# Hybrid attention layer on Trainium2: twelve gate projections move into the stick-breaking groups and pass through HBM, three into the last differential group

## The reference, cut to what matters

```python
proj = jnp.einsum('bsd,de->bse', x, w_in[l])          # 5120 columns = 40 tiles of 128
# columns: qa, ka, va (8 heads), qb, kb, vb (4 heads), gate a (1024), gate b (1024)
ya = _stick_breaking_attention(qa, ka, va)            # sigmoid scores, reversed running product, times v
q1, q2 = _rope(qb[:, :, 0], cos, sin), _rope(qb[:, :, 1], cos, sin)   # and k1, k2
yb = _differential_attention(q1, q2, k1, k2, vb, lam) # softmax(z1) - lam * softmax(z2), times v
yb = _rms_norm(yb, subln_gain[l]) * (1.0 - lam_init)
gate_a = jax.nn.sigmoid(proj[..., c_vb:c_ga])
gate_b = jax.nn.sigmoid(proj[..., c_ga:])
merged = (gate_a * jnp.einsum('bse,ed->bsd', ya, w_branch_a[l])
          + gate_b * jnp.einsum('bse,ed->bsd', yb, w_branch_b[l]))
mix_out = jnp.einsum('bsd,de->bse', merged, w_out[l])
x = _layer_norm(DEEPNORM_ALPHA * x + mix_out, ln1_gain[l], ln1_bias[l])
h = jnp.square(jax.nn.relu(jnp.einsum('bsd,df->bsf', x, w_ff1[l])))
x = _layer_norm(DEEPNORM_ALPHA * x + jnp.einsum('bsf,fd->bsd', h, w_ff2[l]), ln2_gain[l], ln2_bias[l])
```

## Time and profile before

| what | value |
|---|---|
| device time, median of 3 runs | 1707.2 us (1705.44 to 1707.46) |
| profiled execution, first to last instruction | 1700.1 us |
| PE busy in it | 1582.8 us, 93% |
| DVE, ACT, POOL busy | 956.7, 493.3, 458.0 us |
| granted TensorE clock, mean | 0.984 of full speed |

### The profile page before, as it was taken

One profiled execution on the slowest core, in us unless ns is written; L12 is line 12 of the kernel. 1 busy time (PEld: TensorE's weight loads), 2 busy tenths in 40 slices (PEclk: granted clock), 3 DMA queues, 4 the chain that ended last, 5 costly groups with the idle time before them and its releaser, 6 DMA issues.

```text
span 1700.1 us, 21123 instructions
## 1 busy us (share of the span) xinstructions
PE 1582.8 (93%) x7472; PEld 1293.1 (76%) x7472; DVE 956.7 (56%) x1536; ACT 493.3 (29%) x897; POOL 458.0 (27%) x264
## 2 busy tenths in 40 slices
PE   8888887788889889999999999999999999999996
PEld 6666666666777778888878888888888888888885
DVE  3898897988677673121135664444444444444548
ACT  3555565665555442000022221111111111111121
POOL 3544444433222210222230032222222222222313
PEclk9999999999999999999999999999999999999999
DMA  4100100001000000212133131111111111111102
GB/s 162 45 13 26 38 25 13 25 13 38 14 25 25 25 16 23 62 38 59 44 107 99 41 111 47 50 50 50 49 49 49 49 49 49 49 49 49 50 1 99
DMA packets 95209, 79.79 MB, mean 47 GB/s; under 512 B 3248, under 2 KB 85168, under 8 KB 95024
## 3 DMA queue, kind: packets, MB, share of 16 engines
q1 hardware_dynamic: 95152, 79.05, 14.9%
HBM read 74.84 MB, written 4.19 MB: 46 GB/s over the span
## 4 chain that ended last, share of the span: by engine, by line
PE 66%; DVE 16%; issue 12%; POOL 3%; ACT 1%; DMA 1%; DVEq 0%; SPq 0%; POOLq 0%; ACTq 0%
PE p_z L848 6%; PE p_z L850 6%; PE p_z L849 6%; PE p_proj L497 4%; PE p_proj L495 4%; PE p_proj L493 4%; PE p_proj L826 3%; PE p_proj L827 3%; PE p_proj L828 3%; DVE a_t L1205 3%; PE p_z L769 2%; PE p_z L770 2%; PE p_z L771 2%; PE p_z L698 2%; PE p_z L699 2%
## 5 line engine op out<-in xcount | busy, mean ns | idle before, releaser
L493 PE MATMUL p_proj<-xt_h,w_hi 128*128 128x512 f32 x640 | 256.3, 401 | 0.6 <-DVE xt_l L1205 0.6
L497 PE MATMUL p_proj<-xt_h,w_lo 128*128 128x512 f32 x640 | 255.0, 398 | 0.0
L495 PE MATMUL p_proj<-xt_l,w_hi 128*128 128x512 f32 x640 | 253.3, 396 | 0.0
L1594 DVE TENSOR_TENSOR res<-p_z,res 128x512 f32<-128x512 f32 x224 | 150.8, 688 | 109.9 <-PE p_z L850 109.9
L1665 POOL TENSOR_TENSOR w_lo<-w_raw,w_hi 128x1024 fp32r<-128x1024 f32 x48 | 116.6, 2430 | 322.0 <-DVE w_hi L1212 322.0
L1756 POOL TENSOR_TENSOR w_l<-w_raw,w_h 128x1024 fp32r<-128x1024 f32 x31 | 79.5, 2585 | 366.2 <-DVE w_h L1562 366.2
L849 PE MATMUL p_z<-w_l,h_h 128*128 128x512 f32 x448 | 174.3, 389 | 0.0
L850 PE MATMUL p_z<-w_h,h_l 128*128 128x512 f32 x448 | 174.3, 389 | 0.0
L848 PE MATMUL p_z<-w_h,h_h 128*128 128x512 f32 x448 | 174.3, 389 | 0.0
L497 PEld LDWEIGHTS p_proj<-xt_h,w_lo 128*128 128x128 f32 x640 | 122.2, 191 | 23.2
L493 PEld LDWEIGHTS p_proj<-xt_h,w_hi 128*128 128x128 f32 x640 | 122.2, 191 | 22.3 <-DVE xt_l L1205 0.6
(11 more groups left out here) (270 smaller groups left out, 3226.0 us busy)
## 6 DMA issues: line engine op xcount, KB each, us to landing
w_raw<-w_ff SPq DMA_DIRECT2D x64, 512.0 KB, 4.0
w_raw<-w_in SPq DMA_DIRECT2D x40, 512.0 KB, 3.8
y<-x SPq DMA_DIRECT2D x8, 512.0 KB, 8.5
wo_raw<-w_out SPq DMA_DIRECT2D x8, 512.0 KB, 8.0
rows<-x SPq DMA_DIRECT2D x8, 512.0 KB, 3.3
out<-rows_out SPq DMA_DIRECT2D x8, 512.0 KB, 2.6
w_raw<-w_branch_a SPq DMA_DIRECT2D x8, 256.0 KB, 2.8
w_raw<-w_branch_b SPq DMA_DIRECT2D x8, 256.0 KB, 3.2
```

What stands on the lines that cost most here:

```text
L493: pe.matmul(o, w_hi[n_slot][:, k, :], xt_h[:, k, cols], start=(k == 0), stop=False)
L495: pe.matmul(o, w_hi[n_slot][:, k, :], xt_l[:, k, cols], start=False, stop=False)
L497: mm = pe.matmul(o, w_lo[n_slot][:, k, :], xt_h[:, k, cols], start=False, stop=(k == KT - 1))
L1594: dve.tensor_tensor(o, by_block(dn_banks[n % 4]), o, ALU.add).then_inc(dn_added, 1)
```

## The change

A group now has six filler tiles if it is an SB group: the three that the next group needs and three gate tiles. The six halves of those gate tiles go through a sigmoid on ACT (`gate_half`) into three new buffers `gst`, and SP stores each finished gate, 512 KB, to an HBM scratch of twelve rows (`store_gate`). These are gates a and b of column tiles 2 to 7. The last DF group gets three filler tiles (gates a0, b0, a1), and one gate (b1) is left to cover the norm of yb (`last_gate`). In stage 3 the branches follow each other directly; SP brings the stored gates back (`load_gates`), DVE splits the branch weights three column tiles ahead (`split_branch`) over three slots. All counts that the semaphores wait for are rewritten.

```diff
     def tile(self, t):
-        return self.g * 3 + (3 + t)
+        return self.g * 6 + (3 + t) if self.sb else self.g * 3 + (15 + t)
...
+            def store_gate(g, j):
...
+                sp.dma_start(gate_rows[bass.ds(g * 3 + j, 1)].rearrange("a p c -> (a p) c"), gst[j][:, :])\
+                  .then_inc(s_gst, 16)
...
+            def load_group(g, gate_col, qkv_col, store=True):
+
+                for t in range(6):
+                    load_tile(g * 6 + (3 + t), qkv_col(t) if t < 3 else gate_col(t - 3))
+                    if store and 1 <= t < 4:
+                        store_gate(g - 1, t - 1)
...
+            def load_gates(i):
+
+                if i == 2:
+                    sp.wait_ge(s_gst, 12 * 16)
+                    sp.wait_ge(rp_done, 16)
+                else:
+                    sp.wait_ge(m_ready, i - 2)
+                for t in range(2):
+                    sp.dma_start(gate_pairs[i % 3][t][:, :], gate_rows[6 * t + i - 2]).then_inc(gate_in[i % 3], 16)
+
+            load_branch(0)
+            load_branch(1)
+            load_gates(2)
+            for i in range(2, KT):
                 load_branch(i)
-                load_tile(i * 3 + 27, i * P + (GATE_A + P))
-                load_tile(i * 3 + 28, i * P + (GATE_B + P))
-            load_branch(KT - 1)
+                if i + 1 < KT:
+                    load_gates(i + 1)
...
-            attention(Group(0, True, 3, False))
+            attention(Group(0, True, 6, False))
             with pe.Fori(1, SB_GROUPS - 1) as g:
-                attention(Group(g, True, 3, False))
-            attention(Group(SB_GROUPS - 1, True, 3, True))
+                attention(Group(g, True, 6, False))
+            attention(Group(SB_GROUPS - 1, True, 6, True))
...
-            attention(Group(GROUPS - 1, False, 2, False))
+            attention(Group(GROUPS - 1, False, 3, False))
...
-            with pe.Fori(1, KT - 2) as i:
-                branch(i, False, 0)
-                branch(i, False, 1)
-                gates(i)
-            gates(KT - 2)
-            for i in (KT - 2, KT - 1):
+            for i in range(1, KT):
                 branch(i, False, 0)
                 branch(i, False, 1)
...
+                def gate_half(t, h):
+
+                    act.wait_ge(pj_done, G.tile(t) * 2 + (h + 1))
+                    if h == 0 and not (isinstance(g, int) and g == 0):
+                        act.wait_ge(s_gst, g * 48 + 16 * (t - 5))
+                    act.activation(gst[t - 3][:, h * NH:(h + 1) * NH], p_proj[:, h, :], ACT.Sigmoid)\
+                       .then_inc(pj_plain, 1)
...
+            split_branch(2)
+            for i in range(KT - 1):
+                merge(i)
+                if i + 3 < KT:
+                    split_branch(i + 3)
```

More of the change, by code:

```diff
@@ L229, in layer_kernel @@
         x1t_l = at("x1t_l", 96, [P, KT, S], F32R)
-        gate_pairs = [stage[:2], [stage[2], at("gate_b1", 160, [P, S])]]
+        gst = [at(f"gst{j}", 207 + 4 * j, [P, S]) for j in range(3)]
+        gate_pairs = [stage[:2], gst[:2], [gst[2], at("gate_b1", 160, [P, S])]]
         m_h = [at(f"m_h{s}", 176 + 8 * s, [P, KT, P], F32R) for s in range(2)]
@@ L296, in layer_kernel @@
             sem("gate_ready"), sem("br_done"), sem("br_read"), sem("m_ready"))
+        s_gst = sem("s_gst")
+        gate_in = [sem(f"gate_in{j}") for j in range(3)]
         s_gain1, s_gain2 = sem("s_gain1"), sem("s_gain2")
@@ L357, in tile_after @@
         def tile_after(G, k):
-            done = [i // 2 for i in G.halves_at(k) if i in (1, 3)]
+            done = [i // 2 for i in G.halves_at(k) if i % 2 and i < 2 * G.tiles - 1]
+            assert len(done) < 2
             return done[0] if done else None
@@ new lines, in _ @@
+            load_group(0, lambda j: GATE_A + P * (2 + j), lambda t: P + SB_W * t, False)
+            with sp.Fori(1, SB_GROUPS - 1) as g:
+                load_group(g, lambda j: g * (5 * P) + (GATE_A + P * j), lambda t: g * P + (P + SB_W * t))
+            sp.dma_start(cs[:, :, :], rope).then_inc(s_rope, 16)
+            load_group(SB_GROUPS - 1, lambda j: GATE_A + P * (13 + j), lambda t: SB_W * (3 + t))
+            for t in range(3):
+                load_tile(27 + t, P + SB_W * (3 + t))
+                if t:
+                    store_gate(SB_GROUPS - 1, t - 1)
@@ L701, in branch, with last_gate @@
                 mm.then_inc(br_done, 1)
-            def gate(i, t):
+            def last_gate():
+                pe.wait_ge(wt_lo, 40)
                 for h in range(2):
[L706 to L714, removed]
+                    pe.wait_ge(pj_plain, 61 + h)
+                    yield from half_matmuls(0, h, lambda mm: mm.then_inc(pj_done, 1))
             pe.wait_ge(ya_split, 4)
             branch(0, True, 0, lambda: square_sums([3]))
-            next_gate = gate(0, 0)
+            next_gate = last_gate()
             for h in range(4):
@@ L957, in free @@
                                     act.wait_ge(st_pool, g * 2 + 2)
-                            plain(G.tile(t), h, stage[t], free)
+                            if t >= 3:
+                                gate_half(t, h)
+                            else:
+                                plain(G.tile(t), h, gst[0] if G.last and t == 2 else stage[t], free)
+                def gate_half(t, h):
[4 more added lines that the diff above has]
+                       .then_inc(pj_plain, 1)
                 def weights_om(u):
@@ L1083, in _ @@
                 act.activation(y_h[:, 4 + h, :], y[:, 4 + h, :], ACT.Copy).then_inc(yb_hi, 1)
[L1085 to L1095, removed]
-                        act.activation(gate_pairs[par][t][:, h * NH:(h + 1) * NH], p_proj[:, h, :], ACT.Sigmoid)\
-                           .then_inc(pj_plain, 1)
-            gates(0, 1)
-            with act.Fori(1, KT // 2 - 1) as j:
-                gates(j * 2 - 1, 0)
-                gates(j * 2, 1)
-            gates(KT - 3, 0)
-            gates(KT - 2, 1)
+            for h in range(2):
+                act.wait_ge(pj_done, 79 + h)
+                if h == 0:
+                    act.wait_ge(s_gst, 16 * 11)
+                act.activation(gst[1][:, h * NH:(h + 1) * NH], p_proj[:, h, :], ACT.Sigmoid).then_inc(gate_ready, 1)
+            for t, tile in enumerate((stage[0], stage[1], gst[0])):
+                act.wait_ge(pj_plain, 58 + 2 * t)
+                act.activation(tile[:, :], tile[:, :], ACT.Sigmoid).then_inc(gate_ready, 1)
             def wo_high(k):
@@ L1492, in _ @@
             wo_low(6)
-            merge(KT - 1, 1, 0, False)
+            merge(KT - 1)
             dve.wait_ge(mt_hi, 1)
```

151 lines of the change are left out of this document (80 added, 71 removed).

## The result

The changed kernel takes 1627.9 us (median of 4 runs, 1624.28 to 1630.42), the kernel before 1706.3 us (4 runs, 1702.29 to 1707.46): a ratio of 0.955, 95% interval 0.9528 to 0.9571. In a later round, with 5 runs of the changed kernel and 9 of the kernel before, the ratio was 0.9537 (0.9520 to 0.9554). The direction was as forecast, the size was not: 57 us were forecast, 78 came, and 1627.9 lies under the range of 1635 to 1673. The profiled execution has a span of 1623.9 us, 76.2 less than before and 19 under the 1643 that were forecast. The other 3 us of the 22 by which 1627.9 misses 1650 come from the step from span to median: 7.1 us were added, and here it is 4.0.

The account below looks back on a forecast made before the run. PE bounds the kernel, with waits on DVE's `a_t` in SB groups to fill. 54 (SB waits) + 5 (last DF group) - 4 (stage 3) + 2 (clock) = 57 us off 1700.1, span 1643, median 1650; range 1635 to 1673 us.

Parts of the forecast that it names:

- What leaves stage 3: Stage 3: 13 gate tiles of 10.88 us leave, 141.4 us off the path, 130.6 of them to SB groups.
- What comes into the SB groups: SB groups: three gate tiles each, 32.6 us of PE work, soak up waits; 54 us gained net of moved work.
- The worth of a wait: SB groups: 55 listed waits on `a_t`, 53.6 us, plus 0.16 us hidden under each, are worth 62.4 us.
- The waits left over: SB groups: 2 us of waits stay per group, 8 in all, where POOL subtractions and long scans meet.
- The clock: Third and fourth SB groups: part of PE's reduced clock returns with fewer waits, 2 us gained, bounds 0 and 5.
- The side work: SB groups: casts and POOL subtractions raise DVE's load from 69.5 to at most 78.7 us, counted on DVE, not PE.
- The last DF group: Last DF group: one more tile of 10.9 us, with 5 of 7 us of PE waits gone.
- Stage 3 as it is now: Stage 3: load and merge rounds take 10.8 to 12.8 us against PE's 10.88; five rounds cost 4 us.
- A: SB groups: a chain inside each batch keeps half the waits, 31 us gained instead of 54, 1673 us; chance 0.15.
- B: Stage 3: bound by its loads, 13 us lost instead of 4, 1659 us, or 1664 at slower loads; chance 0.10.
- D: SB groups and stage 3: DVE's casts stand waiting for weights, slower kernel, 1764 us at 6.7 us each; chance 0.05.
- C: SB and last DF groups: waits go entirely and the clock comes back, 74 us gained, 1633 us; chance 0.10.

Follow-up runs that it names:

- The doses: Kernel before plus 35, 70, 95 or 145 matmuls by a zero weight tile in each SB group's filler: 1707.8, 1706.2, 1722.0, 1757.5 us.
- zero dose of 145: Kernel before plus 145 matmuls by a zero weight tile in each SB group's filler, without casts, subtractions, sigmoids or stores: 1757.5 us.
- At five: Changed kernel with branch weights first, last merge moved up, and five filler tiles in SB groups 1 to 3, four in DF groups 1 to 3: 1621.2 us.

## Why the prediction was wrong

**What bounds the kernel**: right in kind. The waits on `a_t` were what the filler could take, and they went. They were not all of it.

**What leaves stage 3**: right, 141.4 - 4 forecast, 137.7 measured between the first and last branch matmul.

**What comes into the SB groups**: this is the step that failed. It took what filler can soak up as the listed waits on `a_t` with 0.16 us each, 62.4 us, and put at nothing what PE loses without a row for it. Forecast was that 54 of the 62.4 us of waits are saved, and 2 of clock. Measured, by lengths: 3 x (77.6 + 32.7 - 93.6) + (86.7 + 32.7 - 98.3) = 71.2 us, 15.2 more.

- *The worth of a wait*, the main term: PE lost 77 us at the turns and not 62.4. The 0.16 us were right for the first wait of a turn. Left out were the second one, of the values on `y_sum`, and waits of the transposes too short to be listed. With them 10.2 us more went than the listed waits say, 8.1 and 2.1. The doses show it without any of the change's other parts: it goes with PE work alone.
- *The waits left over*, taken at 2 us per group, 8 in all: 3.7 us listed in 7 places, with the hidden part 4.8, and nearly all in the fourth group. 3.2 us of the miss.
- *The clock*, taken at 2 us: 0.98 and 0.96 in the third and fourth group became 1.00 and 1.00, and the groups without their turns took 3.3 us less in all, 1.3 of the miss. Whether the clock alone would have won even that is not shown. The third group before was no longer than the first two (77.6 us each) though its matmuls took 1.6 us more, since it waited less, 16.6 us at its turns against 18.0 and 18.1. The prediction's bound of 5.0 us counts its 1.5 in full.

Together 14.7 of the 15 us. My bound of 62.4 for "nothing left" was no bound, since it stood on the listed time; that is why the range ended at 1635. PE's own side of a group, put at 96.2 us, fell with it: the first three groups are 93.6 and not 96 to 100. The fourth, 98.3, is in its range.

**The side work**: DVE's load in a group was forecast at up to 78.7 us and is 76 to 78. The sum came out, but its parts are not the forecast ones. The zero dose of 145 has 67.5 to 68 there, so three tiles add some 9.3 us. The six casts take 6.4 us instead of 2.1 for three, 4.3 more and not 2.1, since one of them in each group now stands beside a subtraction of POOL (`k_lo`) and takes four times as long:

```profile
226.12 2.77 DVE L1252 CAST w_hi<-w_raw 128x1024 fp32r<-128x1024 f32 x1
```

```profile
225.45 2.89 POOL L1730 TENSOR_TENSOR k_lo<-stage,k_hi 64x1024 fp32r<-64x1024 f32 x1 [1.80 <-DVE k_hi L1260]
```

The other 5.0 us are DVE's remaining operations, less than the 3 x 2.37 us of the bound. By the Trainium skill's rule (SBUF — State Buffer, Who interferes with whom: an exclusive lock, where the second one to issue blocks) a DVE operation with two SBUF inputs that issues second waits until the subtraction has ended. The trace agrees in single places: beside POOL's subtraction from 156.42 to 158.81 DVE's product of 255 columns took 2.41 us, and 1.06 at the same place with zeros. It does not bear out the full price for every subtraction. In the prediction's own example DVE did not end with POOL but 0.56 us after it (153.63 and 153.07). It was right to put this on DVE and not on PE, at six tiles. At five it would have been wrong.

**The last DF group**: forecast +5.9, measured +4.8; the listed waits went from 6.1 us to 4.1.

**Stage 3 as it is now**: right in place, and near in size. The rounds are some 11.4 us long (the casts stand 11.04 and 11.84 us apart at the start) between the bounds of 10.8 and 12.8, and loading the weights first takes 2.2 to 2.9 us out, where 4 were in the sum. From the merge to the cast it was 6.7 to 7.2 us, near the middle of 6.1 to 8.1.

**The rivals**: A, B and D are out by the waits, by the rounds and by DVE's waits for loads in the SB groups (1.7 us, 3 times). C, given 0.10, came nearest with 1633 us. It had the right direction, the waits entirely gone and the clock back, but it stood on the same 62.4: it has 67.4 us for the SB groups, and 71.2 came although 4.8 us of waits were left. E is out: the groups grew by 16 us and not by 33.

The rest of the miss is small: 1.1 us in the last DF group, 1.1 at `w_out`, 1.6 in the DF groups and 1.7 behind, less 1.5 at the start. The clock's short falls lie differently from run to run there, and a DF group was 69.8 instead of 68.2 us in one trace or another of the same kernel; I take these for scatter.

## What to carry to other kernels

To size what filler can soak up, take the length of a stage and subtract the pace of its matmuls, start to start, rather than add up the listed waits. Here the listed waits gave 62 us, the turns had lost 77, and 68 of them went. It is an upper bound: in the DF groups some 15 us, an estimate, stand over the plain pace, and 11.35 us of work still cost 5.5 to 7.1. Where an engine waits twice in a row, look at both semaphores, since the second wait may have no row. Fill until the waits are gone and a little more: the first 16 us per group cost 2.2 and the last 11 cost 10.6, but the side work that comes with real tiles (casts, subtractions on an engine that blocks another) needs some of that surplus to hide under. And a queue that serves two consumers should carry first what an in-order engine stands waiting for.

## What the runs showed of the hardware that I had not expected

- A turn with no listed wait still cost 0.36 us over a clean one (0.72 against 0.36 from the last filler matmul to the values), and the profile shows PE as busy in it: two waits, each shorter than what is left of the listed matmul before it.
- TensorE's granted clock did not fall once in the four SB groups after the change (1.00 in all four stretches), with the same matmuls that ran at 0.98 and 0.96 in two of them before; in the first three DF groups, with their waits nearly unchanged (28.6 us before, 27.1 now), it stayed at 0.95.
- DVE's load rose by 9.3 us per group for three tiles, of which 4.3 are casts; one cast in each group took 2.77 us beside a subtraction on POOL, where 0.69 is usual.
